# The products with the values ahead of the cumulative sums in every step of stick-breaking attention

## The reference

```python
def stick_breaking_block(q, k, v, q_pos, k_pos):
    z = jnp.einsum('bqhd,bkhd->bhqk', q.astype(jnp.float32), k.astype(jnp.float32)) * (SB_HEAD_DIM ** -0.5)
    mask = k_pos[None, :] < q_pos[:, None]
    log_not = jnp.where(mask, jax.nn.log_sigmoid(-z), 0.0)
    rev = lax.cumsum(log_not, axis=3, reverse=True)
    tail = jnp.pad(rev[..., 1:], ((0, 0), (0, 0), (0, 0), (0, 1)))
    a = jnp.where(mask, jnp.exp(jax.nn.log_sigmoid(z) + tail), 0.0)
    return jnp.einsum('bhqk,bkhd->bqhd', a, v.astype(jnp.float32))
```

## Time and profile before

| | |
|---|---|
| median of 3 runs | 2892.12 us (2883.65 to 2895.70) |
| the profiled execution | 2885.41 us, of which the profile's span is 2883.7 us |
| TensorE matmuls busy | 2831.2 us, 98% of the span |
| VectorE, ScalarE, GpSimdE busy | 44%, 30%, 8% of the span |
| chain that ended last | TensorE 96%, ScalarE 2%, VectorE 2% |
| the same chain by line | L376 85%, L466 4%, L440 2%, L866 1%, L497 1% |
| mean granted TensorE clock | 0.991 of full |

### The profile page before, as it was taken

The page is one execution under the profiler, slowest core; times in us unless marked ns, Lnnn a source line. Parts: engine busy times, 40 slices in busy tenths (PEclk is TensorE's granted clock), DMA queues, the critical chain, the costliest instruction groups (busy, mean ns, idle before and its releaser), DMA issues.

```text
span 2883.7 us, 49404 instructions
## 1 busy us (share of the span) xinstructions
PE 2831.2 (98%) x21250; PEld 2752.5 (95%) x21250; DVE 1262.9 (44%) x1626; ACT 861.7 (30%) x903; POOL 229.2 (8%) x228
## 2 busy tenths in 40 slices
PE   8999999999999999999989899999999999999998
PEld 8987999999999999999989899999999879999998
DVE  4346443333455434334467543333443464433333
ACT  3136432222312322223223432222321364322222
POOL 3000100000111100001133210000010001000001
PEclk9999999999999999999999899999999999999999
DMA  4210232222222222222211122222232102322221
GB/s 152 81 54 1 88 106 88 82 79 88 74 87 78 84 88 88 74 87 88 61 58 59 37 88 84 78 88 76 85 103 73 62 1 75 120 83 78 88 75 61
DMA packets 205498, 223.45 MB, mean 77 GB/s; under 512 B 3750, under 2 KB 200464, under 8 KB 205360
## 3 DMA queue, kind: packets, MB, share of 16 engines
q1 hardware_dynamic: 200992, 206.06, 22.0%
q0 software_dynamic: 4368, 15.38, 1.5%
HBM read 208.56 MB, written 12.86 MB: 77 GB/s over the span
## 4 chain that ended last, share of the span: by engine, by line
PE 96%; ACT 2%; DVE 2%; DMA 0%; issue 0%; POOL 0%; SPq 0%; ACTq 0%
PE bank L376 85%; PE bank L466 4%; PE bank L440 2%; PE bank L608 1%; ACT big L866 1%; PE bank L497 1%; PE bank L433 1%; PE bank L673 0%; PE bank L670 0%; PE bank L657 0%; PE bank L646 0%; PE bank L560 0%; PE bank L393 0%; DMA big<-in_x_prompt 0%; DVE mixs L1144 0%
## 5 line engine op out<-in xcount | busy, mean ns | idle before, releaser
L376 PE MATMUL bank<-ahi,whi 128*128 128x288 f32 x3584 | 771.7, 297 | 6.8 <-DVE alo L1090 6.8
L376 PE MATMUL bank<-ahi,wlo 128*128 128x288 f32 x3584 | 767.6, 296 | 0.0
L376 PE MATMUL bank<-alo,whi 128*128 128x288 f32 x3584 | 767.5, 296 | 0.0
L755 ACT ACTIVATE whi<-raw 128x2048 fp32r<-128x2048 f32 x191 | 364.5, 1908 | 838.3 <-PE bank L376 838.3
L376 PEld LDWEIGHTS bank<-ahi,whi 128*128 128x128 f32 x3584 | 579.1, 189 | 8.9 <-DVE wlo L1065 6.9
L376 PEld LDWEIGHTS bank<-alo,whi 128*128 128x128 f32 x3584 | 578.5, 189 | 0.0
L376 PEld LDWEIGHTS bank<-ahi,wlo 128*128 128x128 f32 x3584 | 578.3, 189 | 0.0
L376 PE MATMUL bank<-hhi,whi 128*128 128x288 f32 x2560 | 548.8, 296 | 7.7 <-DVE hlo L1234 7.7
L376 PE MATMUL bank<-hhi,wlo 128*128 128x288 f32 x2560 | 546.9, 295 | 0.0
L376 PE MATMUL bank<-hlo,whi 128*128 128x288 f32 x2560 | 546.6, 295 | 0.0
L1065 DVE TENSOR_TENSOR wlo<-raw,whi 128x2048 fp32r<-128x2048 f32 x192 | 442.8, 2306 | 207.8 <-ACT whi L755 205.2
(11 more groups left out here) (249 smaller groups left out, 1734.4 us busy)
## 6 DMA issues: line engine op xcount, KB each, us to landing
raw<-in_mlp_w_up SPq DMA_DIRECT2D x64, 1024.0 KB, 5.3
raw<-in_mlp_w_down SPq DMA_DIRECT2D x64, 1024.0 KB, 5.2
raw<-in_sb_w_qkv SPq DMA_DIRECT2D x24, 1024.0 KB, 5.1
raw<-in_conv_w_in SPq DMA_DIRECT2D x12, 1024.0 KB, 5.1
raw<-in_gla_w_in SPq DMA_DIRECT2D x12, 1024.0 KB, 5.3
raw<-in_sb_w_o SPq DMA_DIRECT2D x8, 1024.0 KB, 5.1
out<-mixs POOLq DMA_DIRECT2D x2, 2048.0 KB, 7.7
out<-big POOLq DMA_DIRECT2D x2, 2048.0 KB, 8.3
```

The source lines that it names most:

```text
L376: mm = pe.matmul(acc[h][:, 0:HALF], w[:, u, k, m * P:(m + 1) * P], a[:, k, h * HALF:(h + 1) * HALF], start=(k == 0 and w is whi and a is a ...
L755: act.activation(whi[:, 1 - u], raw[:, 1 - u], ACT.Copy).then_inc(w_hi, 1)
```

## The change

In steps 1 to 23 the two last calls on TensorE change places. In step `k` the products with the values of unit `k - 1` are issued behind the scores of unit `k + 2` and ahead of the cumulative sums of unit `k`. No wait, matmul or DMA is added or taken away, and the programs of the other engines stay as they are.

```diff
                 for k in range(1, UNITS):
                     if k + 2 < UNITS:
                         scores(k + 2)
+                    weighted_values(k - 1)
                     cumulative(k)
-                    weighted_values(k - 1)
                 weighted_values(UNITS - 1)
```

## The result

The changed kernel takes 2956.76 us (median of 4 runs, 2935.58 to 2961.91), the kernel before 2892.23 us; the ratio is 1.0204, 95% interval 1.0178 to 1.0229. A second series gave 2948.71 us (6 runs, 2936.37 to 2950.03) and 1.0209 (1.0169 to 1.0249). It is slower by some 60 us, inside the range of 2932 to 2962; the forecast was 2945. The profiled execution took 2953.15 us, with a span of 2951.4 us against 2883.7.

A forecast was written before the change was run, and what follows sets the result against it. TensorE bounds the kernel: a step costs scores, cumulative sums and exponential, with products free under the exponential. Exposing them: 21.7 + 1.1 + 3.8 = 26.6 us a layer, 53.2 for two; forecast 2945 us, range 2932 to 2962.

The forecast's parts named there:

- small clock case: One 10 us stretch a layer at the lower clock, 5 us of work taking 10; 2955 us; nearly all of 5%.
- output case: Output copies or subtractions slip; kind 0 products stand up to 1.7 us more in six steps; 10 us a layer, 2965; 6%.
- Part 1: Steps 1 to 21: each step is longer by its now uncovered products, 21.7 us a layer.
- Part 2: Kind 0 products wait for the previous pair's output to leave its banks: 0.18 us in six steps, 1.1 us a layer.
- Part 3: Last steps, after unit 21's sums: 14.06 us instead of 10.26, with a 2.68 us wait opening step 22; 3.8 us more.
- Parts 4 and 5: First steps: transposed and cached values arrive in time, no cost. Later units' splits, logs, exponents get more time, giving nothing back.
- The rival with the clock: TensorE's idle in every step lowers its clock: 2955 us in small form, about 3185 if low throughout; chance 5%.
- one of the two signs that I had named for being wrong: In the steady steps: a round of 15.1 us, or a granted clock under 1.00, would make the prediction wrong.
- all else is equal: Changed profile: apart from attention stages 26 to 27 us longer in each layer, nothing else would differ.

The follow-up runs named there:

- experiment 6: Kernel before the change, with most of the value products of kinds 1 and 2 left out; 2865.78 us (one execution).
- experiment 7: Changed kernel, with most of the value products of kinds 1 and 2 left out; 2943.12 us (one execution).
- experiment 8: Changed kernel with the scores of unit k + 2 moved behind the sums of unit k (sums, scores, products); 2889.29 us, ratio 0.9986.
- experiment 3: Changed kernel with seven extra matmuls of 448 columns, results unread, filling the wait in step 22; 2946.40 us (one execution).
- experiment 1: Changed kernel with steps 22 and 23 back in the old order; 2939.82 us, ratio 1.0166.
- experiment 2: Changed kernel with only step 22 back in the old order; 2930.86 us (one execution).
- experiment 9: Kernel ordered sums, scores, products, with ScalarE's logs of unit k + 1 also moved ahead of the weights of unit k - 1; 2900.91 us, ratio 1.0034.
- experiment 5: Changed kernel with the products moved ahead of the scores too (products, scores, sums) in every step; 3022.24 us (one execution).

## Why the prediction was right, and where its sizes were off

*The time.* The sum gave 53 us and the kernel lost some 60; the time is inside the range because the range reached up to take in the small clock case and half of the output case. The first of these happened, the second did not.

*What bounds the kernel, and the mechanism.* Right. Steps cost scores + products + sums + exponential, with the wait of before left in place; experiments 6 and 7 show the cover directly, and experiment 8 shows that the cost goes when something else covers the exponential.

*Part 1, the products.* Predicted 21.7 us a layer at 1.06, 1.03 and 1.01 us. The chain of after has 1.06 for kind 0 in the first round and 1.12 in the later ones, and 1.03 and 1.01 for the others. The Trainium skill's spacing ("TensorE: Matmul & The Clock Gate", "Back-to-back issue gap"), by which products of kind 2 would be an estimated 0.52 us, is not what this trace shows; the four records cost 1.01 us when exposed.

*Part 2, the wait for the pair before.* Predicted 0.18 us in six steps; the chain shows none. It goes from the scores to the products at 211.67 without a stop. Before, ScalarE's copy (L870) started 0.10 us behind the end of the exponential (252.91 against 252.81), 0.04 us behind the products of kind 2; in the timeline of after it starts 0.10 us ahead of that end (228.19 against 228.29). The likely reason is that those products are done long before now; so part of the lag that I carried over was made by their old place: from the end of the exponential to the last subtraction it took 1.67 us, and now takes 1.45 (229.74 against 228.29). Parts 1 and 2 together: 22.8 predicted, 22.1 measured in layer 0. The round: 18.36 predicted, 18.24 measured.

*Part 3, the last steps.* Predicted 14.06 us against 10.26. With the clock kept up (experiment 3) it is 14.16. In the changed kernel it is 19.7 in layer 0 and 18.2 in layer 3. The step was right in its waits and lacked the clock.

*Parts 4 and 5.* No wait showed up for values, cached values or splits.

*The rival with the clock.* I gave it 5%, and it happened in its small form: 5.6 us at the end of layer 0 and about as much in layer 3, where 1.6 us of it lie in one steady round and 4.0 at the end, some 11 us in all. With the 0.7 us a layer by which parts 1 and 2 came out lower, that is the distance from 53.2 to 63.3 us. The step that failed is the argument against it, that the clock of 1.00 in the prologue speaks for a clock of 1.00 in the changed steps. I compared busy shares (2.21 of 4.30 us in the prologue) and held the longest gap there, 1.4 us, for a match for every gap of the change, although part 3 of the same text had put a wait of 2.7 us at step 22. And the row itself was luck: with the same instructions and waits, the clock did fall in that prologue in three of the 24 stages of all the traces (layer 0 of experiments 1, 2 and 9, a granted clock of 0.66 from 190 to 195 us each). A place with the longest single wait and nothing but matmuls behind it is where a fall costs, and it deserved a chance of its own. The Trainium skill's warning (same page, "A second HAM failure mode: psum-queue depth-cycling"), that short idles between groups of matmuls can make the clock swing, is borne out here by the falls in single steady rounds and by experiment 5, after I had put it aside because of one row.

*What was foretold of the profile.* The round (18.24), the busy share (83%), the place of the products, the idle of 1.1 us ahead of the masks, and the wait that opens step 22 (2.55 us) are there; the stages are 31.6 and 31.7 us longer, not 26 to 27. And one of the two signs that I had named for being wrong did show, though not in most rounds: a granted clock under 1.00 in a steady round (0.57 from 2366 to 2370 us). It left the sum nearly as it was, 1.6 us in layer 3, but it says that the argument on the clock was wrong. That all else is equal did not hold either, by 4.4 us.

## What to carry to other kernels

When two engines hand work back and forth, ask of each piece of work what it covers, and not only whether its own input is ready. Here a microsecond of products was worth a microsecond only as long as it stood between the sums and the first instruction that needs their result; issued earlier, it freed nothing and uncovered the wait, 23 times a layer. A change that opens a wait on TensorE should be priced twice, once for the wait and once for the clock in the matmuls behind it.

## What was not expected of the hardware

*The clock.* A wait of 2.55 us brought it from 1.00 to about half in four stages of four; one of 1.7 us in one stage of two. The 1.1 us waits of steady steps, with TensorE 83% busy, did it for some 3 us in one round of each layer 3 stage and in none of layer 0, in the five executions with the new order and all products (the changed kernel twice, experiments 1 to 3). The prologue, with waits of 1.44 and 0.35 us, had a fall in three stages of 24. Seven idle-filling matmuls, 1.69 us of work, kept the clock up in both stages of the one execution that had them. What exactly decides stays open.

*Two speeds at the same granted clock.* The long runs of projection matmuls (3072 of them, 288 columns each) come in two lengths. The chain of waits of before, in layer 1:

```profile
986.77 399.50 PE bank L376 x3072
```

And that of after:

```profile
1017.69 409.58 PE bank L376 x3072
...
2161.23 143.67 PE bank L376 x1104
```

The granted clock is 1.00 in both long runs, and the spacing 0.130 or 0.133 us. Within one execution some such runs have the one and some the other: in the traces of this case none, one or two of the three stretches of 3072 are fast, and experiment 8's execution has two of them and a short one (399.50, 399.50 and 143.67 us). Each long one is worth 10.1 us, the short one 3.5 (143.67 against 147.21 us). The trace of before has one long fast stretch and the trace of after a short one: 10.1 - 3.5 = 6.6 us, which covers the 4.4 us outside the attention to some 2 us.

Over all twelve traces the span without the two attention stages goes from 2605.1 to 2633.1 us. With 10.1 us added for each fast long stretch and 3.5 for each fast short one, it goes only from 2628.8 to 2633.2 us. So these two speeds are most of what differs outside the attention from one traced execution to the next; that they also make the spread of 12 to 28 us between the untraced runs of one kernel is likely, and not shown. What sets the speed of a stretch stays open. A change of a few microseconds in this kernel is to be read from its stage in the trace, not from the total.
